# Norm transposes on the DMA engines instead of TensorE in a two-layer retention and sliding-window step

## The chip, the cores and the metric

The program runs on the 8 cores of one Trainium2 chip, each core with its own prompt sequence and its own 16 decode sequences; the cores exchange nothing. The metric is the device time in microseconds (us) of the slowest core, median of the runs. Lower is better.

## What is computed

Two pre-norm layers over a prompt of 2048 tokens and 64 decode tokens (16 sequences of 4) per core, width 1024. Each layer is a mixer and a gated feed-forward part, each behind its own RMS norm:

```python
h  = x * rsqrt(mean(x*x) + EPS) * gain        # four norms: mix0, ffn0, mix1, ffn1
x += mixer(h)          # layer 0: retention, 4 heads, key 256, value 512, chunks of 128
h  = norm(x)
x += (silu(h @ Wg) * (h @ Wu)) @ Wo           # d_ff = 2816
# layer 1 the same with grouped-query attention over a window of 128
```

The outputs are both streams, the retention states and the key/value caches.

## The kernel before, in words

Everything stays in SBUF for the whole program: `X` (17 tiles of 128 tokens by 1024, f32, tile 16 being the 64 decode tokens), and `HT`, the normed activations transposed, [128, 8, 2112] bf16: model dimension on partitions in 8 blocks, tokens along the row. The matmuls of a stage read `HT` (as the moving or as the stationary operand); the result is added into `X` by VectorE; then the next norm is taken and written into `HT`, tile by tile, over the tile that the stage has finished with.

**The norm of one tile** is `norm_tile(gi, t, part)`, `gi` being which of the four norms. Part "a": ScalarE squares and sums (into `hb`, which serves as scratch), GpSimd makes the inverse root in two small operations (`rsq`, L730 and L726), ScalarE writes the scaled tile in bf16 to `hb`. There are two buffers `hb0` and `hb1`, used in turn. Part "b": eight TensorE transposes of 128 by 128 (`tr`, L711) into one PSUM bank, then one VectorE `tensor_tensor` (`tt`, L726) that multiplies the bank by the gain, which is broadcast along the tokens, and writes `HT`. For the decode tile it is eight transposes of 64 rows.

**The stages.** Retention (0 to about 750 us): four heads one after the other, 16 chunks each; only in the last head (h = 3) does `gn_out` call the next norm's part "a" for a chunk, and part "b" follows a chunk later (`pend_nb`). The same chunks carry one step of a decode sequence each: SyncE's queue loads a 512 KB state (`load_s0`), two buffers, and stores it again (`ss_out`). Each chunk's group norm (`gn_elem`) needs two small GpSimd operations as well. The first feed-forward (to about 1215 us) walks through 6 groups of hidden units, 4, 4, 4, 4, 3, 3 blocks; in each it goes over 4 slices of 512 tokens and the decode tile. After each slice of the last group the norms of its four tiles come together. Attention (to about 1540 us) goes by 16 blocks of 128 tokens: after block n has added into `X` (`o_mm`) comes part "a" for n, and part "b" for n - 1; GpSimd does the rotary additions of the block (two of 128x640) and small table products (128x64). The second feed-forward fills the rest.

**The order of the instructions** on each engine is not the order of the code. `Prog.schedule` is a list scheduler: it simulates all five queues with a duration for each operation (`dur`, from the helpers: a GpSimd `tensor_tensor` costs 0.25 us and 2.2 ns an element of a row, `_vd`), picks for each engine the ready operation with the lowest program number, and also hands out the PSUM banks. A DMA takes 0.1 us of SyncE's queue, starts 1.6 us after its issue or when the one shared pipe is free (`pipe[0]`), moves at `DMA_RATE` = 230e3 bytes a us, and has landed 0.5 us later. `nbytes` counts four bytes an element whatever the type. The queues then run on the chip in this fixed order; each instruction waits for the semaphores of what it depends on, and what stands behind it in its queue waits too. The weights come in by GpSimd's queue as well (cast to bf16 by the DMA).

All operations are recorded by helpers, so that lines of the profile are the helpers': L203 DMA, L705 matmul, L711 transpose, L719 ScalarE, L726 `tensor_tensor`, L730 `tensor_scalar`, L736 `scalar_tensor_tensor`. `R` is all of SBUF and `PS` all of PSUM.

Of the kernel before, what the change touches and what calls it, by code (L numbers as in the profile page):

```python
# [10 lines left out]
ALU = mybir.AluOpType  # L11
# [28 lines left out]
DMA_RATE = 230e3  # L40

class Op:
# [3 lines left out]
    def __init__(self, eng, emit):  # L46
        self.eng = eng
        self.emit = emit
        self.deps = []
        self.idx = -1  # L50
        self.sig = False
        self.sigcnt = 0
        self.slot = None
        self.cnt = 0
        self.is_dma = False
        self.waits = []
        self.pre_slot_wait = 0
        self.seq = 0
        self.dur = 0.3
        self.tbl = None  # L60
        self.reg = 0
        self.vbs = ()
        self.fin = 0.0
        self.st = 0.0
        self.form = 0
        self.know = None
        self.prio = 0
        self.nbytes = 0
# [45 lines left out]
class Prog:  # L114
# [138 lines left out]
    def schedule(self):  # L253
# [31 lines left out]
        prev_ops = [[] for _ in range(8)]  # L285
        cur_tbl = [None]
        last_form = [0]
        pipe = [0.0]
        total = len(allops)
        done = 0  # L290
        stall = {e: 0.0 for e in ENGS}
# [9 lines left out]
        def bank_slot(n, old):  # L301
            best = None
            for b in range(0, 9 - n - (0 if old else RESERVE)):
                if all(owner[b + j] is None for j in range(n)):
                    t = max(free_at[b + j] for j in range(n))
                    waste = 0
                    if n == 1:
                        waste = 0 if (b % 2 == 1 and owner[b - 1] is not None) or (b % 2 == 0 and owner[b + 1] is not None) else 1
                    elif n == 2:
                        waste = b % 2  # L310
                    k = (t, waste, b)
                    if best is None or k < best[0]:
                        best = (k, b)
            return (best[0][0], best[1]) if best else (None, None)
# [50 lines left out]
        while done < total:  # L365
            for e in ENGS:
                if dirty[e]:
                    cache[e] = decide(e)
                    dirty[e] = False
            pick = None  # L370
            for e in ENGS:
                c = cache[e]
                if c is not None and (pick is None or c[2] < pick[0]):
                    pick = (c[2], e, c[1])
            if pick is None:
                left = {e: len(cand[e]) for e in ENGS}
                print("oldest", oldest[0], vbs[oldest[0]].n)
                dn = set(id(x) for e2 in ENGS for x in order[e2])
                for v in {v2.vid: v2 for v2 in owner if v2}.values():
                    rem = [x for x in allops if v in x.vbs and id(x) not in dn]  # L380
                    x = rem[0]
                    print(v.vid, v.n, "left", len(rem), x.eng, x.seq, x.dur, [(d.eng, d.seq, d.is_dma, [w.vid for w in d.vbs]) for d in x.deps if id(d) not in dn][:6])
                raise RuntimeError(f"scheduler stuck {done}/{total} {left} banks {[v.vid if v else None for v in owner]}")
            st, e, o = pick
            cand[e].remove((o.prio, o.seq, id(o)))
            heapq.heapify(cand[e])
            dirty[e] = True
            stall[e] += max(0.0, st - t_eng[e])
            for vb in o.vbs:
                if vb.phys is None:  # L390
                    t, b = bank_slot(vb.n, place.get(vb.vid, -1) == oldest[0])
                    vb.phys = b
                    while oldest[0] < len(vbs) and vbs[oldest[0]].phys is not None:
                        oldest[0] += 1
                    for j in range(vb.n):
                        owner[b + j] = vb
                        for q in prev_ops[b + j]:
                            if q not in o.deps:
                                o.deps.append(q)
                    dirty["pe"] = True  # L400
            if e == "pe":
                if o.form and last_form[0] and o.form != last_form[0]:
                    st += FORM_SW
                last_form[0] = o.form
            if e == "act" and o.tbl is not None:
                if cur_tbl[0] != o.tbl:
                    st += 1.3
                    cur_tbl[0] = o.tbl
            if o.is_dma:
                t_eng[e] = st + (0.95 if e == "pool" else 0.1)  # L410
                s0 = max(st + 1.6, pipe[0])
                pipe[0] = s0 + o.nbytes / DMA_RATE
                fin = pipe[0] + 0.5
            else:
                t_eng[e] = st + o.dur
                fin = t_eng[e] + LAT[e]
            o.fin = fin
            o.st = st
            order[e].append(o)
            done += 1  # L420
            if e == "pe":
                regs[o.reg] -= 1
            for vb in o.vbs:
                vb.left -= 1
                vb.fin = max(vb.fin, fin)
                vb.ops.append(o)
                if vb.left == 0:
                    for j in range(vb.n):
                        owner[vb.phys + j] = None
                        free_at[vb.phys + j] = vb.fin  # L430
                        prev_ops[vb.phys + j] = list(vb.ops)
                    dirty["pe"] = True
            for s_, issue_only in succ[id(o)]:
                k = id(s_)
                tt = st + 0.1 if issue_only else (fin if s_.eng != e or o.is_dma else t_eng[e] + SAME[e])
                if tt > ready[k]:
                    ready[k] = tt
                ndep[k] -= 1
                if ndep[k] == 0:
                    heapq.heappush(cand[s_.eng], (s_.prio, s_.seq, k))  # L440
                    dirty[s_.eng] = True
# [180 lines left out]
class Builder:  # L622
# [3 lines left out]
    def __init__(self, stage=99, debug=False):  # L626
        self.stage = stage
        self.debug = debug
        nc = bass.Bass("TRN2", target_bir_lowering=False)
        self.nc = nc  # L630
        self.P = Prog(nc)
        self.din = {}
        self.dout = {}
        self.uid = 0

    def inp(self, name, shape):
        self.din[name] = self.nc.dram_tensor(name, list(shape), F32, kind="ExternalInput").ap()
        return self.din[name]
# [103 lines left out]
    def pair_out(self, xt, wchunks, reads_of, lhs_of, nk):  # L742
        bi, bk = self.bank(1)
        for i in range(nk):
            for hf in range(2):
                self.mm(self.psf(bi)[hf * NS:(hf + 1) * NS, :], lhs_of(i), wchunks(i)[:, hf * 512:(hf + 1) * 512], i == 0, i == nk - 1,
                        reads_of(i), bk, par=2)
        o = None
        for hf in range(2):
            xv = self.X[0:NS, xt, hf * 512:(hf + 1) * 512]  # L750
            o = self.tt(xv, xv, self.psf(bi)[hf * NS:(hf + 1) * NS, :], ALU.add, [("X", xt)] + bk, [("X", xt)])
        return o

    def recip(self, out, in_, reads, writes):
        return self.P.op("dve", lambda e: e.reciprocal(out=out, in_=real(in_)), reads, writes, dur=self._vd(out, "dve"))
# [34 lines left out]
class Mega(Builder):  # L790
# [113 lines left out]
    def norm_tile(self, gi, t, part="ab"):  # L904
        n = 128 if t < NT else NS
        if "a" in part:
            i = self.norm_cnt % 2
            self.norm_cnt += 1
            self.norm_ctx[t] = i
            hb, hk = self.hbs[i], f"hb{i}"  # L910
            st = self.nst[:, i, :]
            sk = ("nst", i)
            xk = ("X", t)
            x = self.X[0:n, t, :]
            self.act(hb[0:n, :], x, AF.Square, [xk], [hk, sk], scale=D ** -0.5, accum_out=st[0:n, 0:1])
            self.rsq(st[0:n, 1:2], st[0:n, 0:1], n, [sk])
            self.act(hb[0:n, :], x, AF.Copy, [xk, sk], [hk], scale=st[0:n, 1:2])
        if "b" in part:
            i = self.norm_ctx.pop(t)
            hb, hk = self.hbs[i], f"hb{i}"  # L920
            bi, bk = self.bank()
            pb = self.psb(bi).rearrange("p (a b) -> p a b", a=8)
            for c in range(8):
                self.tr(pb[:, c, 0:n], hb[0:n, c * 128:(c + 1) * 128], self.ident[0:n, 0:n], [hk, "ident"], bk)
            self.tt(self.HT[:, :, t * 128:t * 128 + n], pb[:, :, 0:n], self.gainT[:, gi, :].unsqueeze(2).broadcast_to([128, 8, n]), ALU.mult,
                    bk + ["gainT"], [("HT", t)])
# [756 lines left out]
```

How the kernel before makes its waits and increments, by code:

```python
        def run(e, eng):  # L525
            for o in self.ops[e]:
                for (k, v) in o.waits:
                    if k[0] == "eng":
                        eng.wait_ge(self.sems[k[1]], self.ops[k[1]][v].sigcnt)
                    else:
                        eng.wait_ge(self.slot_sems[k[1]], 16 * v)
                ins = o.emit(eng)
                if o.is_dma:
                    ins.then_inc(self.slot_sems[o.slot], 16)
                elif o.sig:
                    ins.then_inc(self.sems[e], 1)
            if e == "sp":
                for s, c in final_slots.items():
                    eng.wait_ge(self.slot_sems[s], 16 * c)
```

## Time and profile before

| | |
|---|---|
| median of 3 runs | 2008.47 us (2007.52 to 2010.4) |
| the profiled execution: its own time | 2006.02 us |
| its span on the slowest core (core 7) | 2004.5 us; all cores 1994.1 to 2004.5 |
| busy, of the span | PE 94%, PEld 44%, VectorE 54%, ScalarE 37%, GpSimd 13% |
| granted TensorE clock, mean of each core | 0.977 to 0.982 |
| DMA | 153.80 MB, mean 77 GB/s |

The span runs from the first to the last instruction; the profiled execution's own time is 1.5 us longer, and the median of the runs another 2.5 us. PE is TensorE's matmuls (and transposes), PEld its weight loads, which overlap them. Busy time is not a measure of what bounds a stage; the chain of waits (who released whom, back from the last instruction) says that.

### The profile page before, as it was taken

What the parts mean: (1) busy time and instruction counts of PE and PEld (TensorE: products, weight loads), DVE (VectorE), ACT (ScalarE), POOL (GpSimd) and SP (SyncE); (2) the same over time, 40 slices, a digit from 0 to 9 for tenths busy, and PEclk for the clock granted to TensorE, in tenths of its full rate; (3) what the DMA queues carried; (4) which work ended last, traced back from release to release, by engine and by line L of the source; (5) the groups of instructions that cost most, each with busy time, mean ns of one, the idle gap of its engine ahead of it and who ended that gap; (6) DMA issues with size and microseconds to landing.
All of it is one profiled execution on the core that took longest, in us unless ns stands there. A gap on an engine that the chain in (4) does not pass through costs nothing.

```text
span 2004.5 us, 30003 instructions; the slowest of 8 cores (1994.1 to 2004.5 us)
## 1 busy us (share of the span) xinstructions
PE 1886.5 (94%) x10850; PEld 876.3 (44%) x10850; DVE 1083.5 (54%) x1544; ACT 740.9 (37%) x1201; POOL 258.7 (13%) x463
## 2 busy tenths in 40 slices
PE   4889999989989989999999998989989999999998
PEld 1434444434434434444444444444444444444444
DVE  3668677767758754334334467665653333343444
ACT  3555454455446761111111155665665111111111
POOL 2211101101111120000000014332331000000000
PEclk9889999999989999999999999999999999999999
DMA  9745743653552450533024113000064031240113
GB/s 183 186 106 133 159 122 112 161 130 125 137 137 103 121 143 15 96 50 64 12 37 60 20 33 64 1 1 4 1 90 64 1 64 22 42 64 0 33 43 132
DMA packets 103823, 153.80 MB, mean 77 GB/s; under 512 B 6464, under 2 KB 56640, under 8 KB 103616
## 3 DMA queue, kind: packets, MB, share of 16 engines
q0 software_dynamic: 59920, 59.91, 20.3%
q1 hardware_dynamic: 43760, 91.97, 13.9%
q8 instruction: 90, 1.47, 0.3%
q14 instruction: 53, 0.43, 0.1%
HBM read 167.08 MB, written 48.76 MB: 108 GB/s over the span
## 4 chain that ended last, share of the span: by engine, by line
PE 84%; DVE 4%; issue 4%; ACT 4%; DMA 2%; POOL 1%; SPq 0%; DVEq 0%; ACTq 0%; POOLq 0%
PE PS L705 81%; ACT R L719 4%; PE PS L711 3%; DVE R L726 3%; DVE R L736 1%; POOL R L726 1%; DMA R<-w_ret_out 1%; DMA R<-w_ffn_in 1%; DMA ss_out<-R 1%; DMA R<-xp 0%; DMA R<-state 0%; POOL R L730 0%; SPq L203 0%; POOL R L203 0%; DVE R L740 0%
## 5 line engine op out<-in xcount | busy, mean ns | idle before, releaser
L705 PE MATMUL PS<-R 128*128 128x512 bf16 (+7 forms) x9568 | 1826.8, 353 | 61.0 <-ACT R L719 32.5
L705 PEld LDWEIGHTS PS<-R 128*128 128x128 bf16 (+3 forms) x9568 | 796.9, 99 | 997.2 <-issue 204.6
L726 DVE TENSOR_TENSOR R<-R,PS 128x1024 f32<-128x1024 f32 (+3 forms) x530 | 484.5, 921 | 616.8 <-PE PS L705 586.1
L719 ACT ACTIVATE R<-PS 128x512 bf16<-128x512 f32 (+7 forms) x674 | 413.0, 626 | 1088.8 <-PE PS L705 999.2
L719 ACT ACTIVATE R<-R 128x1024 bf16<-128x1024 f32 (+3 forms) x302 | 289.3, 972 | 137.1 <-DVE R L726 57.7
L726 DVE TENSOR_TENSOR R<-PS,R 128x1024 bf16<-128x1024 bf16 (+7 forms) x270 | 179.2, 682 | 171.9 <-PE PS L705 105.2
L711 PE MATMUL PS<-R 128*128 128x128 bf16 (+1 forms) x1282 | 127.0, 225 | 50.6 <-ACT R L719 31.3
L736 DVE SCALAR_TENSOR_TENSOR R<-PS,R 128x512 f32<-128x512 f32 (+2 forms) x224 | 137.8, 638 | 59.7 <-POOL R L726 35.7
L726 POOL TENSOR_TENSOR R<-R 128x1 f32<-128x1 f32 (+5 forms) x238 | 150.3, 638 | 108.9 <-DVE R L726 86.4
L736 DVE SCALAR_TENSOR_TENSOR R<-R,PS 128x1024 f32<-128x1024 f32 x124 | 147.7, 1217 | 27.6 <-PE PS L705 17.3
L711 PEld LDWEIGHTS PS<-R 128*128 128x128 bf16 (+1 forms) x1282 | 87.8, 101 | 124.3 <-issue 98.3
L730 POOL TENSOR_SCALAR R<-R 128x1 f32<-128x1 f32 (+1 forms) x136 | 40.0, 294 | 650.3 <-ACT R L719 648.9
L726 DVE TENSOR_TENSOR R<-R 128x512 bf16<-128x512 f32 (+6 forms) x202 | 106.1, 541 | 25.1 <-ACT R L719 14.4
L203 POOL DMA_DIRECT2D R<-w_ffn_in x24 | 21.9, 912 | 603.9 <-PE PS L705 585.6
L719 ACT ACTIVATE R<-PS,R 128x256 bf16<-128x256 bf16 (+2 forms) x76 | 34.5, 453 | 22.0 <-PE PS L705 17.4
L761 DVE TENSOR_REDUCE R<-R 128x20 f32<-128x1280 bf16 (+1 forms) x17 | 25.1, 1474 | 0.0
L203 POOL DMA_DIRECT2D R<-w_ffn_out x12 | 9.2, 763 | 94.7 <-DMA R<-w_ffn_in 75.3
L719 ACT ACT_TABLE_LOAD x13 | 16.7, 1283 | 8.4 <-DMA R<-xp 7.9
L203 POOL DMA_DIRECT2D R<-w_ret_in x16 | 15.0, 938 | 37.1 <-PE PS L705 29.8
L719 ACT ACTIVATION_READ_ACCUMULATOR R<-R 128x1 f32 (+1 forms) x72 | 13.7, 190 | 0.0
L719 ACT ACTIVATION_READ_ACCUMULATOR R<-PS 128x1 f32 x64 | 12.7, 198 | 0.0
L740 DVE COPY R<-R 128x8 bf16<-128x8 bf16 x64 | 10.6, 166 | 3.1
(19 smaller groups left out, 42.2 us busy)
## 6 DMA issues: line engine op xcount, KB each, us to landing
R<-state SPq DMA_DIRECT2D x64, 512.0 KB, 4.3
ss_out<-R SPq DMA_DIRECT2D x64, 512.0 KB, 3.0
R<-w_ffn_in POOLq DMA_DIRECT2D x16, 1024.0 KB, 11.5
R<-xp SPq DMA_DIRECT2D x16, 512.0 KB, 13.8
R<-w_ret_in POOLq DMA_DIRECT2D x8, 1024.0 KB, 12.1
R<-w_ffn_out POOLq DMA_DIRECT2D x8, 1024.0 KB, 9.6
yp<-R SPq DMA_DIRECT2D x16, 512.0 KB, 3.8
R<-w_ffn_in POOLq DMA_DIRECT2D x8, 768.0 KB, 8.9
```

The lines of the kernel that those rows point to most:

```text
L203: return e.dma_start(out=out, in_=in_, **kw)
L705: o = self.P.op("pe", lambda e: e.matmul(real(out), lhsT=lhsT, rhs=rhs, start=start, stop=stop), reads, writes, dur=max(0.029, self._fsz(o ...
L711: o = self.P.op("pe", lambda e: e.transpose(out=real(out), in_=in_, identity=ident), reads, writes, dur=0.057)
L719: return self.P.op("act", lambda e: e.activation(out=real(out), in_=real(in_), func=func, **kw), reads, writes, dur=(0.38 if "accum_out" i ...
L726: return self.P.op(eng, lambda e: e.tensor_tensor(out=out, in0=real(in0), in1=real(in1), op=op), reads, writes, dur=self._vd(out, eng))
L730: return self.P.op(eng, lambda e: e.tensor_scalar(out=out, in0=real(in0), scalar1=s1, scalar2=None, op0=op0), reads, writes, dur=self._vd( ...
L736: return self.P.op(eng, lambda e: e.scalar_tensor_tensor(out=out, in0=real(in0), scalar=scalar, in1=real(in1), op0=op0, op1=op1), reads, w ...
L740: return self.P.op(eng, lambda e: e.tensor_copy(out=out, in_=real(in_)), reads, writes, dur=self._vd(out, eng))
L761: return self.P.op("dve", lambda e: e.tensor_reduce(out=out, in_=in_, axis=AX.X, op=op), reads, writes, dur=0.12 + self._fsz(in_) / 900.0)
```

## The change

Norms 1, 2 and 3 (`gi > 0`: before the first feed-forward, before attention, before the second feed-forward) leave TensorE. Part "b" becomes one transposing DMA from `hb` to the tile's columns of `HT`, issued on SyncE's queue, and one `tensor_tensor` that multiplies these columns by the gain in place: on VectorE for `gi` = 2, on GpSimd for `gi` = 1 and 3. Norm 0 stays as it is. The DMAs use eight semaphores in turn. In the scheduler's simulation they have a pipe of their own at twice the rate.

```diff
-        pipe = [0.0]
+        pipe = [0.0, 0.0]
...
             if o.is_dma:
                 t_eng[e] = st + (0.95 if e == "pool" else 0.1)
-                s0 = max(st + 1.6, pipe[0])
-                pipe[0] = s0 + o.nbytes / DMA_RATE
-                fin = pipe[0] + 0.5
+                pi_ = 1 if o.slot[0] == "xt" else 0
+                s0 = max(st + 1.6, pipe[pi_])
+                pipe[pi_] = s0 + o.nbytes / DMA_RATE / (1 + pi_)
+                fin = pipe[pi_] + 0.5
...
+        self.ndtr = 0
...
+    def dtr(self, out, in_, reads, writes):
+        self.ndtr = (self.ndtr + 1) % 8
+        return self.P.dma("sp", out, in_, slot=("xt", self.ndtr), reads=reads, writes=writes, transpose=True)
...
         if "b" in part:
             i = self.norm_ctx.pop(t)
             hb, hk = self.hbs[i], f"hb{i}"
+            if gi > 0:
+                ht = self.HT[:, :, t * 128:t * 128 + n]
+                self.dtr(ht, hb[0:n, :], [hk], [("HT", t)])
+                self.tt(ht, ht, self.gainT[:, gi, :].unsqueeze(2).broadcast_to([128, 8, n]), ALU.mult, [("HT", t), "gainT"], [("HT", t)],
+                        eng="dve" if gi == 2 else "pool")
+                return
             bi, bk = self.bank()
```

## Rows read from the trace of the kernel before

**Rows 1.** The page of the slowest core, its first lines: span and busy time.
```profile
span 2004.5 us, 30003 instructions; the slowest of 8 cores (1994.1 to 2004.5 us)
...
PE 1886.5 (94%) x10850; PEld 876.3 (44%) x10850; DVE 1083.5 (54%) x1544; ACT 740.9 (37%) x1201; POOL 258.7 (13%) x463
```

**Rows 2.** Busy time by stage: us, PE, PEld, DVE, ACT, POOL, PEclk, DMA share, GB/s.
```profile
569.00:735.00 166.00, 153.46 (x858) 72.40 (x859) 118.53 (x184) 107.83 (x177) 31.66 (x72) 0.94 0.44 124
...
1080.00:1166.00 86.00, 85.74 (x483) 39.70 (x480) 39.32 (x48) 15.35 (x28) 6.78 (x10) 1.00 0.42 65
1166.00:1541.00 375.00, 339.86 (x2504) 165.14 (x2501) 224.90 (x324) 225.99 (x330) 111.11 (x180) 0.98 0.17 26
```

**Rows 3.** The chain of waits, 600 to 680 us: start, duration, what.
```profile
621.69 0.33 PE PS L711 x4
622.02 2.16 PE PS L705 x10
624.17 0.45 PE PS L711 x8
624.62 2.37 PE PS L705 x11
```

**Rows 4.** Timeline of TensorE in the first feed-forward's last group: start, duration, what.
```profile
1165.68 0.61 PE L711 MATMUL PS<-R 128*128 128x128 bf16 x8
1166.13 3.19 PE L705 MATMUL PS<-R 128*128 128x512 bf16 x14
...
1170.69 11.62 PE L705 MATMUL PS<-R 128*128 128x512 bf16 x53
```

**Rows 5.** Groups by shape: count, busy us, mean ns of one, idle time before.
```profile
L726 DVE TENSOR_TENSOR R<-R,PS 128x512 bf16<-128x512 bf16 x176 | 120.7, 688 | 429.6 <-PE PS L705 422.5 <-ACT R L719 5.6 <-POOL R L730 1.4
...
L726 DVE TENSOR_TENSOR R<-PS,R 128x1024 bf16<-128x1024 bf16 x64 | 77.5, 1219 | 45.6 <-PE PS L711 45.4
...
L726 DVE TENSOR_TENSOR R<-R 128x512 bf16<-128x512 f32 x96 | 66.5, 706 | 5.1
...
L726 POOL TENSOR_TENSOR R<-R 128x640 f32<-128x640 f32 x32 | 49.5, 1546 | 12.5 <-DVE R L726 12.5
...
L726 POOL TENSOR_TENSOR R<-R 128x64 f32<-128x64 f32 x64 | 20.9, 327 | 72.8 <-DVE R L726 69.4 <-PE PS L705 3.0
```

**Rows 6.** DMA issues: count, KB of each, median us from issue to landing.
```profile
R<-state SPq DMA_DIRECT2D x64, 512.0 KB, 4.3
ss_out<-R SPq DMA_DIRECT2D x64, 512.0 KB, 3.0
R<-w_ffn_in POOLq DMA_DIRECT2D x16, 1024.0 KB, 11.5
...
R<-c_band POOLq DMA_DIRECT2D x1, 64.0 KB, 2.4
```

**Rows 7.** Timeline of ScalarE in one chunk of the last retention head.
```profile
622.11 0.60 ACT L719 ACTIVATE R<-PS 128x512 bf16<-128x512 bf16 x1 [0.45 <-PE PS L711]
622.61 1.14 ACT L719 ACTIVATE R<-R 128x1024 bf16<-128x1024 f32 x1
...
627.09 0.60 ACT L719 ACTIVATE R<-PS 128x512 bf16<-128x512 f32 x1 [0.79 <-PE PS L705]
```

**Rows 8.** Timeline of GpSimd, the same chunk.
```profile
624.50 0.30 POOL L730 TENSOR_SCALAR R<-R 128x1 f32<-128x1 f32 x1 [2.22 <-ACT R L719]
624.94 0.57 POOL L726 TENSOR_TENSOR R<-R 128x1 f32<-128x1 f32 x1
629.26 0.22 POOL L730 TENSOR_SCALAR R<-R 128x1 f32<-128x1 f32 x1 [3.75 <-ACT R L719]
```

**Rows 9.** Timeline of SyncE's queue, the same chunk.
```profile
623.09 0.37 SPq L203 DMA_DIRECT2D ss_out<-R  x1
625.93 0.38 SPq L203 DMA_DIRECT2D R<-state  x1
```

**Rows 10.** Waits in the attention stage: us in total, times, the longest.
```profile
PE PS L705 <- ACT R L719: 18.2, 25, 2.0
```

## The prediction

> **What bounds the kernel now.** First the page and its busy times [rows 1]: TensorE is busy for 94% of a span of 2004.5 us, VectorE for 54%, GpSimd for 13%. So work taken off TensorE can shorten the run, but only in stages where TensorE is what everything waits for. Next the busy time by stage [rows 2], for the three stretches that hold the norms that change. The last retention head (569 to 735 us) has TensorE busy for 153.46 of 166 us; the last group of the first feed-forward part starts in 1080 to 1166 us, busy for 85.74 of 86; attention and its surroundings have 339.86 of 375. The feed-forward is TensorE alone; attention is not, and its waits say so: matmuls waited 18.2 us for ScalarE [rows 10]. Third, the chain of waits in the retention head [rows 3]: within the steady chunks it is TensorE all the way, and the eight transposes of a norm stand on it with 0.45 us, between two pieces of matmuls. The timeline of TensorE in the feed-forward gives the same: the eight start at 1165.68 and the next matmul at 1166.13 [rows 4], 0.45 us a tile. The mean duration of one transpose is longer, since they overlap, and must not be multiplied by eight.
>
> **What leaves TensorE.** Three norms of 17 tiles, 51 groups of 0.45 us (the three decode tiles cost at most that): 23.0 us if every group stood on the path. In the feed-forward's last group all 17 do: 7.65. In the retention head the chain shows them on the path in steady chunks, but the head also has stretches in which VectorE or a state DMA is last, so I take half: 3.8. In attention TensorE idles for 35 of 375 us and each block waits for ScalarE; half again: 3.8. Sum 15.3 us. One PSUM bank a tile is also no longer needed; I cost that at nothing.
>
> **What moves on VectorE and GpSimd.** The multiplication from PSUM is 1.219 us each, 64 of them [rows 5], 16 in each norm. 32 of the 48 that change leave VectorE (39 us of its busy time); it is not the bound of either stage, so I take nothing for it. The 16 of norm 2 stay on VectorE but read SBUF with a gain in f32; the nearest rows, 128x512 from PSUM at 688 ns and from SBUF with f32 at 706 ns [rows 5], differ by 3%: no change. On GpSimd 128x64 takes 327 ns and 128x640 takes 1546 ns [rows 5], that is 2.12 ns an element: 1024 elements are about 2.36 us, 32 times, 76 us more on an engine that works 31.66 of 166 and 111.11 of 375 us in the two stages [rows 2]. The time is there; what matters is what stands behind it in the queue.
>
> **What the DMA brings.** 48 transfers of 256 KB and three of 128 KB, each with one issue on SyncE's queue and a landing that the multiplication waits for. No row shows a transposing DMA. The bounds are landings in this trace [rows 6]: 2.4 us for 64 KB (c_band) below, 11.5 us for 1024 KB (w_ffn_in) above. The state stream is nearest, as it uses the same queue, 128 partitions and no cast: 3.0 us stores, 4.3 us loads, of 512 KB. I take 4.3 us, since a transpose has half the bytes in much smaller pieces. The scheduler reckons with 1.6 + 524288 / 460000 + 0.5 = 3.2 us and so lays every multiplication about 1.1 us too early in its queue.
>
> The Trainium skill, "Advanced Engine Details and Errata", section X-Bar Transpose (TRN2), says that transposing DMAs are as fast as regular ones there; by it the landing would lie near the 3 to 4 us of the state stream, and the sum would stay as it is or gain the last 3 us that I take off below.
>
> **Where the late landing matters.** On GpSimd in the retention head. The scaled tile is written at 622.61 + 1.14 = 623.75 [rows 7], and the next norm's inverse root starts on GpSimd at 629.26 [rows 8], after idling 3.75 us. A multiplication laid ahead of it must start by 629.26 - 2.36 = 626.90, so the landing may take 3.15 us. Beyond it the inverse root is late, then ScalarE's scaling, and behind that, in ScalarE's queue, the copies that free PSUM banks and feed the matmuls. ScalarE idles 0.45 + 0.79 = 1.24 us in this chunk [rows 7], which absorbs the delay up to a landing of 4.4 us. At 4.3 the cost is just nothing; but the store and the load of a state (issues at 623.09 and 625.93 [rows 9], landings of 3.0 and 4.3) are nearly always in flight with it, and so I take 0.2 us a chunk, 16 times, 3.2 us. The issues on SyncE's queue (0.37 us for an ordinary one [rows 9]) find it free between load and next store; if a transposing one took 2 us it would still fit, and a state load behind it has its second buffer as cover. In the feed-forward's last group VectorE waits for landings, but TensorE has several PSUM banks to write on; cover about one pair of banks, 16 matmuls, 3.2 us for 14 [rows 4]. Norms read by the next stage: its first tiles were normed tens of us earlier, its last are read late; nothing.
>
> **Sum:** -15.3 + 3.2 = -12.1 us. The profiled execution of 2006.0 would become 1994; it stands 2.5 us below the median of the runs (2008.5), which I shift by the same: **1996.5 us**.
>
> **Rivals.** *GpSimd's queue becomes the bound (slower).* The place is the one above: multiplications that wait for their landing, with the small operations of the norms (and, in attention, the rotary additions of 128x640) behind them. Beyond 4.4 us each us of landing costs 16 us in the retention head; break-even is 15.3 / 16 = 0.95 us later, a mean landing of 5.3 us. At 6.5 us the head loses 16 x 2.1 = 34, net +18: about 2027 us. For it: the scheduler's 3.2 us is shorter than I think the landing is, DMA is busy for 44% of that head [rows 2], state stores and loads share the queue, and GpSimd's in-order queue has no other cover. Against: a 512 KB store lands in 3.0 us, and the scheduler may lay the multiplication behind the inverse root instead.
>
> *The landing is of another order.* If the eight blocks of a tile are transposed one after the other, landings reach the upper bound, 11.5 us: 16 x (11.5 - 4.4) = 114 in the retention head alone, and the two `hb` buffers, held until the DMA has read them, also hold ScalarE in the feed-forward, where four tiles come together: about 2008 - 15 + 114 = 2107 us. Against it stands every SyncE row. The Trainium skill, "VectorE: DVE Perf Modes", section The three transpose paths, speaks for it: it gives 1309 ns for a 128x128 block by DMA against 390 ns on TensorE; eight in a row would be 10.5 us. No row here shows it, and TensorE's eight took 0.45 us together.
>
> *No change.* TensorE's time goes, but in the retention head and attention the next wait fills it (ScalarE's share, the state DMAs), and the new order of the queues costs what the feed-forward gains: 2005 to 2012 us. For it: attention's idle TensorE; against: the feed-forward's 7.65 us have nothing else to hide in.
>
> *It does not transpose in one piece,* but element by element: some hundreds of us slower. Little speaks for it.
>
> **How the numbers follow.** Forecast case 0.49 (with a range of its own of 1985, all 23 us, to 2003), no change 0.13, GpSimd's queue 0.28, landing of another order 0.07, not in one piece 0.03. A measurement of this kernel can tell some 0.2%, 4 us, from nothing. Faster is the forecast case and a sliver: 0.49; same 0.13; slower 0.28 + 0.07 + 0.03 = 0.38. The range takes in the forecast, no change and the GpSimd case to 7 us of landing: 1985 to 2030; outside are the last two and a little more.
>
> **What would show it.** Right: the transposes of L711 are 408 fewer, SyncE shows 51 more issues with landings of 3 to 5 us, the feed-forward's last group is shorter by 1.8 us a slice, GpSimd's busy time rises to about 335 us. Wrong: ScalarE or TensorE waiting for GpSimd in 600 to 735 us, idle TensorE there beyond the present 12.5 us, landings above 5.3 us, or state loads that come late because a transposing issue stands before them.

## The result: slower, 2046 us instead of 2008 us

| | before | after |
|---|---|---|
| time, median of 4 runs each, us | 2008.0 (2005.8 to 2010.4) | 2046.1 (2045.2 to 2048.0) |
| ratio, 95% interval | | 1.0191 [1.0173, 1.0208] |
| the profiled execution, us | 2006.0 | 2048.0 |
| its span, us | 2004.5 | 2046.5 |

The forecast was 1996.5 us, with a range to 2030. The time lies 16 us above the range, and the sign is the other one. Some executions run with half of the cores at a lower granted clock and take longer, whatever the kernel; medians and ratios leave them out as far as they can be told apart.

The page of the changed kernel, its busy times, its chain and two of its groups:

```profile
span 2046.5 us, 29069 instructions; the slowest of 8 cores (2031.1 to 2046.5 us)
...
PE 1866.8 (91%) x10260; PEld 857.1 (42%) x10442; DVE 1062.8 (52%) x1510; ACT 736.7 (36%) x1199; POOL 327.7 (16%) x497
...
PE 75%; DMA 8%; DVE 5%; issue 5%; ACT 4%; POOL 3%; SPq 0%; DVEq 0%; ACTq 0%; another core or an unknown queue 0%; POOLq 0%
...
L728 POOL TENSOR_TENSOR R<-R 128x1 f32<-128x1 f32 (+5 forms) x272 | 214.2, 796 | 189.9 <-DMA R<-R 97.7
...
L713 PE MATMUL PS<-R 128*128 128x128 bf16 (+1 forms) x874 | 95.9, 228 | 56.4 <-DVE R L728 26.9
```

Beside [rows 1] the span is 42 us longer. The 1866.8 us of PE can't be set against 1886.5: this page is of core 0, whose trace has 10260 matmul records for 10442 weight loads, so 182 are missing. On the six cores with all records (1 to 5 and 7, in both traces) the median busy time is 1884.5 us before and 1873.6 after. TensorE works 11 us less, and that and the added span have become idle time. The transposes are 874 where the page of before has 1282, 408 fewer. GpSimd does 69 us more, and it waited for "DMA R<-R" for 97.7 us. DMAs are 8% of the chain of waits, 2% on the page of before. R<-R is a DMA from SBUF to SBUF, and in this kernel only the transposes are that.

The DMA issues of the changed kernel, over the whole run (KB aren't given for a transpose):

```profile
R<-R SPq DMA_TRANSPOSE x51, 3.1
```

Their median landing is 3.1 us, where the forecast took 4.3 and the kernel's own scheduler reckons with 3.2. So the typical transpose is no disappointment. What the median hides is the tail of the distribution. The 51 transposes of core 0, each with what the trace shows in flight beside it:

```
in the chunks, alone or beside state traffic     12 (norm 1)   3.0 to 5.6 us
beside a load of w_ffn_out or w_ffn_in (norm 1)   4            11.5, 9.8, 9.9, 4.6 us
norm 2, first 13 tiles                           13            3.0 to 4.3 us
norm 2, beside w_swa_out and w_ffn_in             2            14.6, 16.2 us
norm 3, middle of attention                      12            3.0 to 3.1 us
beside weight and cache loads (norm 3)            4            10.1, 4.9, 5.7, 9.8 us
```

(The four left over are one more of norm 1, at 4.5 us just behind a weight load, the last two of norm 2 and one of norm 3, between 2.8 and 3.2 us.)

**Where the time went** is read from marks that every variant has: the starts of certain DMA issues in the one profiled execution of each variant, median over the eight cores; a stage is the difference of two such medians. A runs from the third store of the prompt state (about 549 us) to the first load of w_ffn_in after 780 us, and holds norm 1. C is the last group of the first feed-forward part, from the last pair of loads of w_swa_in to the first load of w_swa_out (norm 2, less its last tiles). D goes on to the store into vp (the prompt's attention, norm 3 but its last tiles), E to the pair of w_ffn_in loads that stands at 1598 us on core 0 of the kernel before (the cached attention and the start of the second feed-forward part).

```
us          A (norm 1)   C (norm 2)   D (attention)   E      sum    to before
before      267.4        72.2         247.9           141.6  729.1
after       283.1        73.9         256.1           154.8  767.9  +38.8
```

The body of the feed-forward between A and C is 324 us in both, and what follows E is 396 us in both. The change loses in all four stages that it touches, 15.7, 1.7, 8.2 and 13.2 us.

The chain of waits in stage A, core 0 (start, duration, what):

```profile
669.10 1.16 ACT R L721
670.33 5.21 DMA R<-R
675.66 0.42 POOL R L728
676.09 1.55 issue
677.63 0.57 POOL R L732
678.34 0.58 POOL R L728
679.00 1.16 ACT R L721
680.22 11.53 DMA R<-R
691.89 1.89 POOL R L728
693.78 0.30 POOL R L732
694.22 0.58 POOL R L728
```

It is a loop. ScalarE scales a tile (679.00), its transpose lands after 11.53 us, GpSimd multiplies (1.89 us), and only then do the inverse root of the next norm (L732, L728) and the work that hangs on it come. In [rows 3], a chunk of the same head, the chain is TensorE's matmuls and transposes; in these 25 us TensorE isn't in it. (Not all of that is new: in the kernel before, the chain of core 0 leaves TensorE at 683 us too, for 14 us of a state store and a state load.) The waits of that stretch, 569 to 760 us (total us, times, longest):

```profile
POOL R L728 <- DMA R<-R: 56.5, 14, 11.5
...
ACT R L721 <- POOL R L728: 26.4, 11, 7.9
DVE R L738 <- POOL R L728: 23.8, 11, 7.8
```

GpSimd stands for 56.5 us before multiplications whose tile has not landed. ScalarE then waits 26.4 us for GpSimd, longest 7.9, and VectorE 23.8, longest 7.8. In the kernel before, the same window had

```profile
ACT R L719 <- POOL R L726: 7.8, 11, 1.4
DVE R L736 <- POOL R L726: 7.1, 8, 2.2
```

about as often, but never over 2.2 us. The largest single hole is at the start of attention. The chain of waits there, then the timelines of SyncE, TensorE, VectorE and ScalarE (start, duration, what, in brackets the idle time before and what ended it):

```profile
1241.24 1.70 SPq L203
...
1243.03 16.20 DMA R<-R
```

```profile
1241.24 21.57 SPq L203 DMA_TRANSPOSE R<-R  x3
...
1261.83 5.44 PE L707 MATMUL PS<-R 128*128 128x512 bf16 x16 [13.07 <-DVE R L728]
...
1256.32 1.23 DVE L728 TENSOR_TENSOR R<-R 128x1024 bf16<-128x1024 bf16 x1 [11.68 <-DMA R<-R]
...
1255.96 1.06 ACT L721 ACTIVATE R<-R 128x1024 bf16<-128x1024 f32 x1 [11.90 <-DMA R<-R]
```

Two transposes are issued at 1241 and 1243 us, while three loads of w_swa_out and one of w_ffn_in are in flight. VectorE stands at the multiplication of the first for 11.68 us, ScalarE at the next scaling for 11.90, as the two `hb` buffers are still being read by the DMAs, and TensorE for 13.07 us behind VectorE. The chain names it: "DMA R<-R" is 49.8% of 1236 to 1275 us.

TensorE pays a second time after such holes. The windows of core 0 (columns as in [rows 2]; the last number but two is the granted clock):

```profile
730.00:740.00 10.00, 4.64 (x12) 1.15 (x10) 2.44 (x2) 2.10 (x5) 4.49 (x9) 0.50 1.00 240
740.00:760.00 20.00, 17.12 (x74) 6.98 (x77) 7.76 (x14) 11.79 (x18) 6.36 (x10) 0.83 0.34 93
```

In 730 to 740 us, with TensorE busy for 4.64 of 10 us, the granted clock was 0.50, the lower level of 1.2 GHz, and it was 0.83 on the mean of the next 20 us; over the whole run core 0 stands at 0.963 instead of 0.982. How many of the 38 us are this clock and how many the holes themselves isn't separated.

### The profile page after: what moved, and what is told of

It reads as the page before. It is cut to its first block, busy times and chain, and to the rows that moved or that the text cites. A ratio compares the mean times of both kernels' runs of the same rounds, so it can differ in the third digit from the quotient of the medians.

```text
span 2046.5 us, 29069 instructions; the slowest of 8 cores (2031.1 to 2046.5 us)
## 1 busy us (share of the span) xinstructions
PE 1866.8 (91%) x10260; PEld 857.1 (42%) x10442; DVE 1062.8 (52%) x1510; ACT 736.7 (36%) x1199; POOL 327.7 (16%) x497
## 2 busy tenths in 40 slices
DMA packets 156141, 166.73 MB, mean 81 GB/s; under 512 B 58784, under 2 KB 108960, under 8 KB 155936
## 3 DMA queue, kind: packets, MB, share of 16 engines
q1 hardware_dynamic: 96080, 104.95, 17.9%
## 4 chain that ended last, share of the span: by engine, by line
PE 75%; DMA 8%; DVE 5%; issue 5%; ACT 4%; POOL 3%; SPq 0%; DVEq 0%; ACTq 0%; another core or an unknown queue 0%; POOLq 0%
PE PS L707 73%; ACT R L721 4%; DMA R<-R 4%; DVE R L728 3%; POOL R L728 2%; PE PS L713 2%; DMA R<-w_ret_in 2%; DVE R L738 1%; DMA R<-w_ffn_in 1%; DMA R<-w_ret_out 1%; POOL R L732 0%; DMA R<-cv 0%; DMA ss_out<-R 0%; POOL R L203 0%; DVE R L742 0%
## 5 line engine op out<-in xcount | busy, mean ns | idle before, releaser
L707 PE MATMUL PS<-R 128*128 128x512 bf16 (+5 forms) x9386 | 1822.4, 355 | 116.8 <-ACT R L721 41.0
L728 DVE TENSOR_TENSOR R<-R,PS 128x1024 f32<-128x1024 f32 (+3 forms) x530 | 483.9, 921 | 632.3 <-PE PS L707 594.6
L728 POOL TENSOR_TENSOR R<-R 128x1 f32<-128x1 f32 (+5 forms) x272 | 214.2, 796 | 189.9 <-DMA R<-R 97.7
L728 DVE TENSOR_TENSOR R<-PS,R 128x512 bf16<-128x512 f32 (+5 forms) x219 | 120.8, 565 | 164.2 <-PE PS L707 116.5
L728 DVE TENSOR_TENSOR R<-R 128x512 bf16<-128x512 f32 (+7 forms) x219 | 141.2, 660 | 50.9 <-DMA R<-R 20.1
L713 PE MATMUL PS<-R 128*128 128x128 bf16 (+1 forms) x874 | 95.9, 228 | 56.4 <-DVE R L728 26.9
L732 POOL TENSOR_SCALAR R<-R 128x1 f32<-128x1 f32 (+1 forms) x136 | 44.8, 329 | 581.7 <-ACT R L721 579.9
L713 PEld LDWEIGHTS PS<-R 128*128 128x128 bf16 (+1 forms) x874 | 63.3, 102 | 120.9 <-issue 97.5
L742 DVE COPY R<-R 128x8 bf16<-128x8 bf16 x64 | 10.8, 169 | 3.3
```

What stands on the lines that cost most here:

```text
L707: o = self.P.op("pe", lambda e: e.matmul(real(out), lhsT=lhsT, rhs=rhs, start=start, stop=stop), reads, writes, dur=max(0.029, self._fsz(o ...
L713: o = self.P.op("pe", lambda e: e.transpose(out=real(out), in_=in_, identity=ident), reads, writes, dur=0.057)
L728: return self.P.op(eng, lambda e: e.tensor_tensor(out=out, in0=real(in0), in1=real(in1), op=op), reads, writes, dur=self._vd(out, eng))
L732: return self.P.op(eng, lambda e: e.tensor_scalar(out=out, in0=real(in0), scalar1=s1, scalar2=None, op0=op0), reads, writes, dur=self._vd( ...
L742: return self.P.op(eng, lambda e: e.tensor_copy(out=out, in_=real(in_)), reads, writes, dur=self._vd(out, eng))
```

## The experiments

Two theories at first: the late landings are what costs, wherever a transpose meets a weight load; or it is the order of the queues, since the changed scheduler gives the transposes a pipe of their own and so believes in a landing of 3.2 us whatever else is in flight. Against both stands the plain rival that the multiplications cost as such. Twelve kernels were run, on three chips; each ratio is to runs of the kernel before on the same chip. The stages are compared by the marks above, always with the one profile of the kernel before. The intervals of e9 to e12 (third chip) are up to 2% wide, so for those four kernels the stages say more than the ratios.

Every variant is scheduled anew, so the order of all queues changes with it, and with the order what the scheduler puts in: ScalarE loads its function tables 13 times in the kernel before, 11 times in the changed one, 13 in e5 and 15 in e6. The stages show how much that can be. E lies between 140.3 and 148.7 us in the five variants in which none of its tiles goes by DMA (e1, e2, e4, e8, e12; before 141.6); A lies between 267.2 and 269.1 us where norm 1 stays on TensorE. A few us in E alone are therefore no evidence.

All variants start from the changed kernel. Most change the condition `if gi > 0:` in `norm_tile`, which chooses the tiles that go by DMA.

**One norm at a time.** e1 as shown, e2 with `gi == 2`, e3 with `gi == 3`.

```diff
-            if gi > 0:
+            if gi == 1:
```

> Only norm 1 (last retention head) is transposed by DMA; norms 2 and 3 as before. In the changed kernel the stretch from the last head to the first weight issue of the first feed-forward's second group was 14 us longer (median of the cores). Theory A (collision): a transposing DMA lands in 3.1 us alone and in 5 to 12 us when a 1 MB weight load or two state transfers are in flight, and the loss is that excess; about 2008 + 14 = 2022 us, and the tiles that land in 3 us cost nothing. Theory B (every wait of 3 us on an in-order queue costs, whatever else is in flight): 17 of 51 tiles, a third of 38 us, about 2021 us; here both give the same total and differ in where it is lost: A at the four tiles with late landings, B evenly. If GpSimd's multiplication is the cause, the loss is also even.

> Only norm 2 (last group of the first feed-forward) is transposed by DMA, with the multiplication on VectorE. Theory A: 13 of its 17 tiles land in about 3.2 us and are nearly free, two meet the loads of w_swa_out and w_ffn_in and take 15 us; the hole at the stage's end costs some 13 us: about 2020 us, and the four slices before it are within 1 us of before. Theory B: the slices carry the loss evenly, a total of about 2021 us with no hole. The expected saving of TensorE time (7 us) alone would give 2001.

> Only norm 3 (attention) is transposed by DMA, with the multiplication on GpSimd. Theory A: the twelve tiles of the middle land in 3.04 us and gain up to 0.45 us each, the last four and the decode tile meet loads of weights and caches and lose: +13 - 4, about 2017 us. Theory B: even loss over the blocks, about 2021 us.

```
              ratio                      A      C     D      E      sum to before
e1, norm 1    1.0138 [1.0094, 1.0181]    287.4  71.8  249.7  140.3  +20.1
e2, norm 2    1.0101 [1.0056, 1.0147]    267.7  74.6  253.3  145.8  +12.3
e3, norm 3    0.9939 [0.9901, 0.9976]    269.1  72.2  237.3  147.4   -3.1
before                                   267.4  72.2  247.9  141.6
```

Norm 1 costs 20 us in its own stage. Norm 2 costs 2.4 in its own and 5.4 in the next, where its last tiles meet the loads of w_swa_out; another 4.2 are in E, where it has no tile. Norm 3 gains 10.6 us in attention, far more than the 3.8 of the forecast, where both theories expected a loss, and gives back 5.8 in E, where its last tiles meet the cache loads. The three sum to +29 of the 39: most of the loss is local, and some 9 us come only with all three together.

**Only the tiles whose transposes meet nothing.** e4 as shown, e8 with `gi == 3 and t < 12`.

```diff
-            if gi > 0:
+            if gi > 0 and t < (9 if gi == 1 else 12):
```

> DMA transposes only for tiles that met no weight or cache load in the changed kernel (norm 1: tiles 0 to 8, norms 2 and 3: tiles 0 to 11; 33 of 51), TensorE for the others as before. Theory A: the loss is gone, 2008 us or less, down to 1998 (33 x 0.45 saved, less what the slices lose). Theory B: 33/51 of 38 us stay, about 2033 us.

> DMA transposes only for norm 3, tiles 0 to 11, which met nothing; TensorE for all else. With norm 3 whole the attention stage was 10.6 us shorter up to the end of its blocks and lost 5.8 us after it, where five tiles met loads. Theory A: the gain stays and the loss goes: 0.4 to 0.6% below before, 1996 to 2000 us where before has 2008. Theory B: no better than the whole norm 3, 2001 us or more.

e4 measured 1.0045 [1.0003, 1.0086], its stages 272.6, 78.4, 236.5 and 144.1 (+2.5 in sum). Without the tiles that collide, 36 of the 39 us are gone. But it isn't the gain that TensorE's time should give: C is 6.2 us longer, though no transpose in it is late. e8 measured 0.9948 [0.9928, 0.9967], stages 267.5, 72.1, 237.2 and 142.2 (-10.1): it keeps the whole gain of norm 3 in D and loses 0.6 in E instead of 5.8. That fits collisions as norm 3's loss, but E also moves by that much with the order alone, and the ratios of e3 and e8 are the same within their intervals.

**No multiplication (e5).**

```diff
-                self.tt(ht, ht, self.gainT[:, gi, :].unsqueeze(2).broadcast_to([128, 8, n]), ALU.mult, [("HT", t), "gainT"], [("HT", t)],
-                        eng="dve" if gi == 2 else "pool")
```

> The changed kernel without the multiplication by the gain after the DMA transposes of norms 1 to 3 (left out; norm 0 keeps its own). If the multiplications and what waits behind them on GpSimd and VectorE are the cause of the loss, the time returns to about 2008 us or below. If the landings that meet weight loads are the cause (theory A), most of the loss stays: 2030 us or more, since ScalarE still waits for the buffers and the readers for the tiles.

Measured 0.9965 [0.9954, 0.9976], stages 265.5, 68.2, 240.6 and 149.0 (-5.8). All 51 transposes go by DMA and some are as late as before (8.5, 8.3 and 10.7 us in stage A of core 0, 19.3 us beside the loads of w_swa_out), but nothing on GpSimd or VectorE waits for them, and the loss is gone. ScalarE still waits for buffers that late transposes are reading, in all for longer than the 20.0 us of the changed kernel (total us, times, longest):

```profile
ACT R L721 <- DMA R<-R: 27.2, 6, 16.4
```

With late landings alone as the cause it would have been 2030 us or more; it is 2001.2 (median). The multiplications' own time doesn't explain 44 us: the 32 on GpSimd take 1.9 us each, on an engine that is busy for 16% of the span. What fits is that an engine with other work in its queue stands and waits at them; as e5 has a new order too, e6 is the cleaner test.

**One pipe in the scheduler (e6).** The two counters of the simulated DMA become one again, so a transpose behind a weight load is reckoned late, and at the common rate.

```diff
-                pi_ = 1 if o.slot[0] == "xt" else 0
+                pi_ = 0
```

> The changed kernel with one pipe in the scheduler's simulation again, so that it reckons with transposes that queue behind weight and state transfers. Theory A: it lays fewer dependents ahead of the late landings, and part of the 38 us comes back, 5 to 20 us (2025 to 2040); the transfers themselves still meet, so not all. If the order plays no part, 2046 us.

Measured 0.9954 [0.9938, 0.9969], median 1998.0 us: faster than before, where 2025 to 2040 us were expected. The edit touches only the simulation. On the chip the instructions are the same but for four more table loads on ScalarE; what differs is their order in the queues and the PSUM banks that the scheduler hands out with it. The late landings are all still there: 9.3, 10.8 and 8.7 us in stage A, and 15.5 and 16.9 us for the two issued at 1223 and 1225 us, the second with an issue of 9.7 us. SyncE's queue and TensorE at that point, core 0:

```profile
1223.18 11.25 SPq L203 DMA_TRANSPOSE R<-R  x2
...
1219.40 15.92 PE L707 MATMUL PS<-R 128*128 128x512 bf16 x66
```

TensorE runs 15.92 us without a hole, to 1235.3 us, while the same two late transposes are in flight that cost it 13.07 us in the changed kernel; until the second has landed, at 1241.6, its holes are of 0.3 to 1.3 us. VectorE has the rotary work of the prompt ahead of the late tiles' multiplications:

```profile
1226.41 2.36 DVE L728 TENSOR_TENSOR R<-PS,R 128x1024 f32<-128x1024 f32 x2 [3.47 <-ACT R L721]
...
1251.76 1.29 DVE L728 TENSOR_TENSOR R<-R 128x1024 bf16<-128x1024 bf16 x1
```

The waits of stage A (569 to 760 us) changed in the same way:

```profile
POOL R L728 <- DMA R<-R: 14.7, 7, 4.7
ACT R L721 <- POOL R L728: 11.0, 13, 1.7
...
DVE R L738 <- POOL R L728: 8.6, 11, 1.6
```

14.7 us of waiting where the changed kernel has 56.5, and the waits that pass it on are back below 1.8 us. In the chain of waits of core 0, 650 to 745 us, "DMA R<-R" is 33.8% in the changed kernel and isn't among the fourteen largest lines in e6, though three transposes of 8.7 to 10.8 us fall into it. So neither theory is right by itself: without the collisions (e4) the loss is gone, and with them but in another order (e6) it is gone too. A late landing costs where the order has put an engine's next work behind it; the two lines of the simulation are worth 46 us of the stages' sum (from 721.8 to 767.9).

**Which half of the simulation (e9, e10).** e6 changed two things, the shared pipe and the rate. e9 keeps the pipe of their own at the common rate, e10 shares the pipe at twice the rate for transposes.

```diff
e9
-                pipe[pi_] = s0 + o.nbytes / DMA_RATE / (1 + pi_)
+                pipe[pi_] = s0 + o.nbytes / DMA_RATE
e10
-                pi_ = 1 if o.slot[0] == "xt" else 0
+                pi_ = 0
-                pipe[pi_] = s0 + o.nbytes / DMA_RATE / (1 + pi_)
+                pipe[pi_] = s0 + o.nbytes / DMA_RATE / (2 if o.slot[0] == "xt" else 1)
```

> The changed kernel; in the scheduler's simulation the transposes keep a pipe of their own, but at the common rate, so that each is reckoned at 4.4 us instead of 3.2 and never behind a weight load. The kernel with one pipe (4.4 us, and behind the others) took 1998 us against 2046. If it is the margin of 1.1 us for every tile that healed it, this one also comes to about 2000. If it is that the simulation knows of transposes behind weight loads, the loss at the collisions stays: 2025 us or more, less what the ordinary tiles lose.

> The changed kernel with one pipe for all DMAs in the simulation, but the transposes at twice the rate (3.2 us alone, as it is measured). If knowing of the collisions is what heals, about 1998 us, the same as with one pipe and the common rate. If it was the margin, 2030 us or more.

```
                               A      C     D      E      sum to before
own pipe, twice the rate       283.1  73.9  256.1  154.8  +38.8   (the change)
own pipe, common rate (e9)     276.7  68.2  248.3  148.9  +13.0
shared, twice the rate (e10)   275.5  69.2  242.1  147.1   +4.8
shared, common rate (e6)       273.4  68.5  236.0  143.9   -7.3
```

The ratios are 1.0027 [0.9955, 1.0099] and 1.0025 [0.9931, 1.0119], too wide to tell the two apart. By the stages both halves matter: 1.1 us more of reckoned landing takes 26 us off, the shared pipe 34, both 46. Which half does more isn't shown: with the stages taken core by core and the median last, e9 and e10 come to +8 and +6. The shared pipe gives most in D (14 us), whose first tiles meet the loads of w_swa_out.

**Four buffers in the feed-forward's last group (e7).** `hb` holds the scaled tile until its DMA has read it, and there are two.

```diff
-            i = self.norm_cnt % 2
+            i = self.norm_cnt % (4 if gi == 2 else 2)
```

(with `hb2` and `hb3` allocated for that stage, and `nst` for four.)

> The changed kernel with four buffers of normed tiles instead of two in the last group of the first feed-forward, where four norms come together. In the run with norm 2 alone the slices there took 18.4 to 19.1 us instead of 17.4 to 17.7, though all landed in 3.1 to 3.4 us. If the two buffers, held for a landing, are the cause, the slices fall to 16.5 to 17.5 us and the total by 4 to 8 us, to about 2040; the collision at the end of that stage stays. If VectorE's in-order wait for the landing is the cause, no change: 2046 us.

Measured 1.0160 [1.0143, 1.0178]. C is 66.8 us, 7.1 shorter than in the changed kernel and 5.4 shorter than before; the rest is as it was, 283.3, 255.3 and 155.0. So in this order the two buffers were the bound of that stage, and VectorE's wait for the landing, the rival of the expectation, was not its bound. The timeline of TensorE shows what goes, first the changed kernel:

```profile
1187.31 17.71 PE L707 MATMUL PS<-R 128*128 128x512 bf16 x79 [0.64 <-DVE R L728]
1205.74 2.75 PE L707 MATMUL PS<-R 128*128 128x512 bf16 x12 [0.72 <-DVE R L728]
1210.39 10.74 PE L707 MATMUL PS<-R 128*128 128x512 bf16 x48 [1.90 <-DVE R L728]
1221.38 2.54 PE L707 MATMUL PS<-R 128*128 128x512 bf16 x11 [0.25 <-DVE R L728]
1225.20 3.22 PE L707 MATMUL PS<-R 128*128 128x512 bf16 x28 [1.28 <-DVE R L728]
1230.67 0.63 PE L707 MATMUL PS<-R 128*128 128x64 bf16 x16 [2.25 <-DVE R L728]
```

and with four buffers:

```profile
1154.35 42.90 PE L707 MATMUL PS<-R 128*64 128x512 bf16 x195 [0.49 <-DVE R L728]
1197.47 21.51 PE L707 MATMUL PS<-R 128*128 128x512 bf16 x109 [0.22 <-DVE R L728]
```

From 1187 us to the end of the stage the holes of the changed kernel, with one of 0.51 us behind these, add up to 7.55 us; with four buffers there are 0.22, 0.24 and 0.51 us, 0.97 in all. The difference of 6.6 us is nearly the 7.1 that C is shorter. That ScalarE had stood for a buffer is in the waits of the changed kernel, 1166 to 1240 us; with four buffers this wait is not among the nine largest:

```profile
ACT R L721 <- DMA R<-R: 5.9, 4, 1.9
```

**Norms 2 and 3 with the common pipe (e11), and of those only the tiles below 12 (e12: `gi > 1 and t < 12`).**

```diff
-                pi_ = 1 if o.slot[0] == "xt" else 0
+                pi_ = 0
-            if gi > 0:
+            if gi > 1:
```

> One pipe, and DMA transposes for norms 2 and 3 only; norm 1 stays on TensorE. With one pipe and all three norms the retention head and the entry to the feed-forward were 6 us longer than before, the rest 13 us shorter. If the stages add up, 13 us below before, 0.993 to 0.995 of it.

> As the last, but only tiles 0 to 11 of norms 2 and 3 by DMA, those that met no weight load. If with one pipe the colliding tiles still cost something, faster than the last by 1 to 4 us (about 0.992); if the order hides them, the same.

e11: 0.9924 [0.9865, 0.9983], stages 267.2, 66.5, 233.7 and 143.8, -17.9 in sum, by the stages the best of all (by the ratios e3, e6, e8, e11 and e12 overlap); cores 0 to 3 span 1978.1 to 1983.2 us, where the same cores in the profile of before span 1994.1 to 2003.8. e12: 0.9943 [0.9867, 1.0020], stages 268.8, 68.8, 234.1 and 148.7, -8.7. With the common pipe no gain is seen from leaving the colliding tiles to TensorE: e12 is 2.3 us worse than e11 in C and 4.9 in E. That it is really worse isn't shown; e8, with the same tiles of norm 3, has 142.2 in E. And in C, e11 gets its 5.7 us with two buffers, so four aren't needed in this order.

## Why the prediction was wrong

**TensorE's time: the counts right, the sum about right.** 408 transposes left, as said. Busy time fell by 11 us in the changed kernel, with a granted clock of 0.966 instead of 0.980 on the cores compared, and by 21 us in e6 (1863.1 us on the same cores, clock 0.977), against 23.0 in the forecast. For the stages the forecast was -3.8, -7.65 and -3.8. The -7.65 leaned on [rows 4] rightly; the window to 1166 us that was shown with it (85.74 of 86 us busy) ends where the norms of that core begin. Where little waits for a landing, C gives -5.7 (e11) and attention -10.6 (e3). The last was undersized: I took half of TensorE's own time because ScalarE is what attention waits for. Stage D of core 1 before and in e3, with TensorE's waits in it:

```profile
1215.70:1462.40 246.70, 222.07 (x1588) 106.97 (x1586) 157.98 (x241) 148.76 (x228) 84.33 (x132) 0.98 0.09 14
...
PE PS L705 <- ACT R L719: 15.1, 21, 2.0
PE PS L711 <- DVE R L726: 3.9, 6, 1.7
PE PS L705 <- DVE R L726: 2.5, 5, 0.7
```

```profile
1214.10:1451.40 237.30, 215.60 (x1489) 100.05 (x1488) 157.77 (x229) 148.26 (x229) 107.32 (x143) 0.97 0.16 28
...
PE PS L713 <- DVE R L728: 10.5, 12, 1.7
PE PS L707 <- ACT R L721: 9.0, 9, 2.1
```

Of the 9.4 us of this core 6.5 are TensorE's own time: it came back whole for the 12 tiles, not by half. Its waits fall by 3.0 us in all, those for ScalarE by 6, while those for VectorE rise by 4. Why the waits for ScalarE fall isn't separated: the PSUM banks that the transposes no longer take and VectorE's 1.22 us a tile both went, and "I take nothing for it" was said of both.

**The multiplications: right.** VectorE's in place takes 1.23 us (forecast: no change from 1.22), GpSimd's 1.90 us (2.36, scaled from f32; it is bf16). GpSimd's busy time is 328 us (335).

**The landing: the step that failed.** The term was +3.2 us for the retention head, 0.2 us a chunk, which with the -3.8 of TensorE made -0.6; the stage measured +15.7 (and +20.0 in e1). "I take 4.3 us" put one number in the place of a distribution, and multiplied it by 16 chunks. The median, 3.1, is better than that; the mean of norm 1's 17 tiles on core 0 is 4.95 us, as four stand beside weight loads, at up to 11.5. The rival had its break-even at a mean landing of 5.3 us. The mean stayed below, and the stage lost 15.7 us all the same: in the order of this kernel nothing covers a wait of 11 us, and the slack that the early landings leave can't be saved up for it. The row was there: [rows 6] has w_ffn_in at 11.5 us, and it was used as a bound on the transpose's size, not as the transfer that the transpose would have beside it. The forecast looked for neighbours in SyncE's queue (state stores and loads) and not in GpSimd's, whose loads were in flight at every landing over 8.2 us in all the traces. And it took the order for given: with the same landings (mean 4.95 us again on core 0) e6 loses 6.0 us in this stage, not 15.7.

**"Norms read by the next stage ... nothing": failed too.** The argument was that the reader comes late. True, and of no help: it is not the tile's reader that waits, but whatever stands behind the tile's multiplication on VectorE and GpSimd. At 1243 to 1261 us that is attention's first work. D and E lost 8.2 and 13.2 us where the forecast had -3.8 for both.

**"Cover about one pair of banks ... 3.2 us": wrong buffer.** With four `hb` buffers TensorE's holes in C were 0.97 us, so PSUM was enough. What ran out was `hb`, named in the forecast only under a rival, and only for landings of 11.5 us. It ran out at 3.1 us already, in bursts of four tiles: C went to +1.7 instead of -7.65, and to -5.4 with four buffers (and, in the order of e11, to -5.7 with two).

**The rival "GpSimd's queue becomes the bound"** is what happened in the retention head, in its place and by its mechanism, as the chain shows. Its price (+18 us) and its condition (a mean) were both wrong, and it knew nothing of VectorE's and ScalarE's part. "The scheduler's 3.2 us is shorter than I think the landing is" was put as a fault of 1.1 us in every tile. The fault is none in most tiles and 7 to 13 us in a few. But reckoning every tile 1.1 us later, with no knowledge of the collisions, also took back 26 of the 39 us (e9); with the shared pipe on top (e6) the loss of 38 us became a gain of 9.

**The two pages.** The Trainium skill, "Advanced Engine Details and Errata", section X-Bar Transpose (TRN2), says that transposing DMAs run as fast as regular ones. The trace comes near it for one that is alone: 3.04 us, beside 3.0 us for a state store of twice the bytes, and with an issue of 1.23 us instead of 0.37 [rows 9]. The Trainium skill, "VectorE: DVE Perf Modes", section The three transpose paths, has 1309 ns for one block, which makes 10.5 us for eight as an estimate; the trace doesn't agree, since all eight land within those 3.04 us. The late landings near 10 us look like its figure and are something else: they appear only where loads are in flight.

**What stays open.** Why norm 1 costs even in e6: with the common pipe A is 6 us longer than before, and without norm 1 (e11) it is not. On core 0 most of it is in 716 to 760 us, where TensorE is busy for 31.83 us in e6 and for 39.41 before, but no run took it apart. Why C is longer in e4 and E in e12 is open as well, and so are the 9 us that the three norms cost together beyond their sum, and the part of the clock.

## What to carry to other kernels

Before a step is moved from an engine to a DMA, lay its issue times over every other transfer of the core, on whatever queue, and price the worst landings one by one; a mean landing says little about an in-order queue. Then ask of each consumer what stands behind it on its engine, not who reads its result. And where a scheduler's model orders the queues, an optimistic latency there can cost more than the latency itself: nearly the same instructions, with transfers as late, ran 2.4% apart (1.0191 and 0.9954 of the kernel before).

## What the runs showed of the hardware

- A DMA transpose of 128 x 1024 bf16 from SBUF to SBUF lands in 3.04 us when alone; the 12 in attention's middle take 3.04 to 3.09 us. The 51 of them make many small packets: 58784 under 512 bytes on the slowest core's page, before 6464.
- Issued while a weight load of 512 KB to 1 MB was under way it landed in 4.6 to 16.9 us (core 0 of the changed kernel and of e6), and its issue, 1.23 us when alone, took up to 9.7 us of SyncE's queue.
- With TensorE busy for 4.64 us of 730 to 740 us the granted clock was 0.50 (1.2 GHz), and 0.83 on the mean of the next 20 us; it was 0.50 again in 1255 to 1260 us, without a matmul, and 0.72 in 1260 to 1270.
- GpSimd multiplies 128 x 1024 bf16 in place, the gain broadcast along the free axis, in 1.90 us. By [rows 5] 128 x 640 f32 takes 1.55.
